# Turning normed rows by plain transpositions of rows that VectorE has scaled, in a two-layer hybrid decoder trunk

## What is computed

```python
def rms_norm(x, gain=None):
    xf = x.astype(jnp.float32)
    y = xf * lax.rsqrt(jnp.mean(xf * xf, axis=-1, keepdims=True) + EPS)
    if gain is not None:
        y = y * gain.astype(jnp.float32)
    return y.astype(x.dtype)

def hybrid_layer(x, ln_mix_pre, w_in, ..., ln_mlp_pre, w_up, w_down, ln_mlp_post):
    h = rms_norm(x, ln_mix_pre)
    ... = split_projection(h @ w_in)
    ...
    x = x + rms_norm(merged @ w_out, ln_mix_post)
    h2 = rms_norm(x, ln_mlp_pre)
    ff = jnp.square(jax.nn.relu(h2 @ w_up)) @ w_down
    return x + rms_norm(ff, ln_mlp_post)
```

## Time and profile before

| | us |
|---|---|
| median of 3 runs | 2002.19 (2001.02 to 2003.47) |
| the profiled execution | 2001.97 |
| its span | 2000.2 |
| TensorE busy | 1928.5 |
| VectorE busy | 1067.6 |
| GpSimd busy | 1024.3 |
| ScalarE busy | 474.2 |

### The profile page before, as it was taken

The page is one execution under the profiler, slowest core; times in us unless marked ns, Lnnn a source line. Parts: engine busy times, 40 slices in busy tenths (PEclk is TensorE's granted clock), DMA queues, the critical chain, the costliest instruction groups (busy, mean ns, idle before and its releaser), DMA issues.

```text
span 2000.2 us, 25269 instructions
## 1 busy us (share of the span) xinstructions
PE 1928.5 (96%) x8926; PEld 1552.1 (78%) x8926; DVE 1067.6 (53%) x1686; ACT 474.2 (24%) x923; POOL 1024.3 (51%) x821
## 2 busy tenths in 40 slices
PE   8999999999999999999999999999999999999998
PEld 7876667788778888888878667677887788888887
DVE  5754798743464550363366547987435646403623
ACT  3153243221323100011222533523113241000111
POOL 5663443335670666666346534342456607666662
PEclk9999999999999999999999999999999999999999
DMA  6332112222520322222222311122125204222321
GB/s 241 133 122 68 56 61 71 80 74 74 200 95 1 138 95 95 95 98 92 84 85 95 127 58 64 63 72 79 64 74 210 84 1 147 94 95 97 102 93 57
DMA packets 72475, 186.77 MB, mean 93 GB/s; under 512 B 18304, under 2 KB 30784, under 8 KB 71488
## 3 DMA queue, kind: packets, MB, share of 16 engines
q1 hardware_dynamic: 41328, 152.10, 22.2%
q10 hardware_dynamic: 31056, 33.38, 5.0%
HBM read 174.40 MB, written 11.06 MB: 93 GB/s over the span
## 4 chain that ended last, share of the span: by engine, by line
PE 77%; DVE 15%; ACT 4%; issue 3%; POOL 1%; DMA 0%; DVEq 0%; SPq 0%; POOLq 0%; ACTq 0%
PE psD L1008 19%; PE psD L1009 19%; PE psD L1010 19%; PE psM L1008 3%; PE psM L1009 3%; PE psM L1010 3%; DVE work L2047 3%; DVE small L2045 3%; PE psM L1067 2%; PE psM L1074 2%; PE psM L1164 1%; PE psM L1172 1%; DVE x L1946 1%; POOL w_lo L982 1%; ACT wide L1508 1%
## 5 line engine op out<-in xcount | busy, mean ns | idle before, releaser
L982 POOL TENSOR_TENSOR w_lo<-raw,w_hi 128x1024 fp32r<-128x1024 f32 x272 | 672.8, 2473 | 22.7
L1008 PE MATMUL psD<-a_hi,w_hi 128*128 128x512 f32 (+2 forms) x1488 | 601.3, 404 | 10.0 <-DVE a_lo L2170 6.6
L1010 PE MATMUL psD<-a_hi,w_lo 128*128 128x512 f32 (+2 forms) x1488 | 578.4, 389 | 0.0
L1009 PE MATMUL psD<-a_lo,w_hi 128*128 128x512 f32 (+2 forms) x1488 | 578.3, 389 | 0.0
L977 POOL TENSOR_TENSOR w_hi<-raw,tabs 128x1 fp32r<-128x1 f32 x272 | 62.7, 230 | 916.9 <-PE psD L1010 806.7
L1008 PEld LDWEIGHTS psD<-a_hi,w_hi 128*128 128x128 f32 (+1 forms) x1488 | 281.9, 189 | 89.8 <-issue 30.2
L1009 PEld LDWEIGHTS psD<-a_lo,w_hi 128*128 128x128 f32 (+1 forms) x1488 | 281.9, 189 | 59.7 <-issue 5.7
L1010 PEld LDWEIGHTS psD<-a_hi,w_lo 128*128 128x128 f32 (+1 forms) x1488 | 281.5, 189 | 58.8 <-issue 0.4
L978 POOL TENSOR_SCALAR w_hi<-raw 128x1023 fp32r<-128x1023 f32 x272 | 297.8, 1095 | 0.0
L2200 DVE TENSOR_TENSOR f_lo<-gt,f_hi 128x512 f32 x64 | 127.4, 1990 | 59.3 <-ACT f_hi L1766 59.3
L1766 ACT CAST f_hi<-gt 128x512 f32 x64 | 39.8, 622 | 479.7 <-DVE gt L2197 479.7
(11 more groups left out here) (268 smaller groups left out, 2720.7 us busy)
## 6 DMA issues: line engine op xcount, KB each, us to landing
raw<-in_ws SPq DMA_DIRECT2D x272, 512.0 KB, 3.2
s_raw<-in_wo ACTq DMA_DIRECT2D x14, 512.0 KB, 11.4
out<-x SPq DMA_DIRECT2D x8, 512.0 KB, 5.5
x<-rows_d ACTq DMA_DIRECT2D x4, 1024.0 KB, 6.8
x<-out ACTq DMA_DIRECT2D x2, 2048.0 KB, 8.2
e_raw<-in_wo ACTq DMA_DIRECT2D x8, 512.0 KB, 6.5
tabs<-in_tab SPq DMA_DIRECT2D x1, 2944.0 KB, 11.4
x<-in_x SPq DMA_DIRECT2D x4, 512.0 KB, 5.3
```

Of the source, the lines that this page charges most:

```text
L982: pool.tensor_tensor(w_lo[:, s, :], raw[:, s, :], w_hi[:, s, :].bitcast(F32), ALU.subtract) \
L1008: pe.matmul(out, lhi, rhi, start=start, stop=False)
L1009: pe.matmul(out, lhi, rlo, start=False, stop=False)
L1010: return pe.matmul(out, llo, rhi, start=False, stop=stop)
```

## The change

`diagonal` becomes `scaled`. VectorE now multiplies the tile of `x` itself by the column of scales, in two halves of 128 by 512, and writes all of `wide[:, t]`; each half raises a semaphore. TensorE turns blocks of `wide` by plain transpositions (a matmul in transpose mode, with the identity as its other operand), and waits for the half that it needs. The order of the halves follows the order in which TensorE turns the blocks: channels 4 to 7 first in front of the projections, save for the last tile, and channels 0 to 3 first everywhere else. In the MLP's turn the wait for the scales moves into the loop over the halves.

```diff
-            def diagonal(norm, t, of=None):
+            def scaled(norm, t, of=None):
 
                 r = rstd(norm, t, 1, of)
-                sig(dve.tensor_scalar(wide[:, t, 0:P], T("ident"), r, None, ALU.mult), "diag_" + norm)
+                for half in (0, 1) if norm == "pre_mlp" or t == ST - 1 else (1, 0):
+                    w = slice(half * S, (half + 1) * S)
+                    sig(dve.tensor_scalar(wide[:, t, w], x[:, t, w], r, None, ALU.mult), "rows_" + norm)
...
         def scaled_T(pe, ps, t, k):
-            return pe.matmul(ps[:, cut(t)], x[:, t, cut(k)], wide[:, t, 0:P], start=True, stop=True)
+            return pe.transpose(ps[:, cut(t)], wide[:, t, cut(k)], T("ident"))
 
         def activation_T(pe):
             for t in range(ST):
-                pe.wait_ge(*on("diag_pre_mix", t + 1))
-                for k in range(KT) if t == ST - 1 else (4, 5, 6, 7, 0, 1, 2, 3):
+                for i, k in enumerate (range(KT) if t == ST - 1 else (4, 5, 6, 7, 0, 1, 2, 3)):
+                    if i % (KT // 2) == 0:
+                        pe.wait_ge(*on("rows_pre_mix", 2 * t + i // (KT // 2) + 1))
...
                     def turn_x1(t):
-                        pe.wait_ge(*on("diag_pre_mlp", t + 1))
                         for i in range(2):
+                            pe.wait_ge(*on("rows_pre_mlp", 2 * t + i + 1))
...
-                                ins = pe.matmul(x1_T(t, k), x[:, t, cut(k)], wide[:, t, 0:P], start=True, stop=True)
+                                ins = pe.transpose(x1_T(t, k), wide[:, t, cut(k)], T("ident"))
```

More of the change, by code:

```diff
@@ L594, in build @@
         per_layer = {"slab_done": NSLAB, "split": NSLAB, "a_hi": (2 + ST) * KT, "a_lo": (2 + ST) * KT,
-                     "h_turned": KT, "r_pre_mix": ST, "diag_pre_mix": ST}
+                     "h_turned": KT, "r_pre_mix": ST, "rows_pre_mix": 2 * ST}
         def sem(name):
@@ L741, in rstd @@
                 return cols[6]
-            def diagonal(norm, t, of=None):
+            def scaled(norm, t, of=None):
                 r = rstd(norm, t, 1, of)
-                sig(dve.tensor_scalar(wide[:, t, 0:P], T("ident"), r, None, ALU.mult), "diag_" + norm)
-            return total, rstd, diagonal
+                for half in (0, 1) if norm == "pre_mlp" or t == ST - 1 else (1, 0):
+                    w = slice(half * S, (half + 1) * S)
+                    sig(dve.tensor_scalar(wide[:, t, w], x[:, t, w], r, None, ALU.mult), "rows_" + norm)
+            return total, rstd, scaled
         def signals(eng, who):
@@ L967, in _ @@
                 seen, sig, own = signals(dve, "dve")
-                total, rstd, diagonal = dve_norm(dve, sig, own)
+                total, rstd, scaled = dve_norm(dve, sig, own)
                 dve.wait_ge(kept["basics_in"], 16)
                 for t in range(ST):
-                    diagonal("pre_mix", t)
+                    scaled("pre_mix", t)
             @block.gpsimd
@@ L2183, in _ @@
                             lo_x1(READY - 1)
-                        diagonal("pre_mlp", t)
+                        scaled("pre_mlp", t)
                         if t == READY - 1:
@@ L2254, in _ @@
                         if t and layer < DEPTH - 1:
-                            diagonal("pre_mix", t - 1, layer + 1)
+                            scaled("pre_mix", t - 1, layer + 1)
                         r = rstd("post_mlp", t, 2)
@@ L2260, in _ @@
                     if layer < DEPTH - 1:
-                        diagonal("pre_mix", ST - 1, layer + 1)
+                        scaled("pre_mix", ST - 1, layer + 1)
                 if layer == DEPTH - 1:
```

## The result

The changed kernel takes 2012.49 us (median of 22 runs) against 2004.3 us for the kernel before (22 runs beside it). The ratio is 1.0036, with a 95% interval of 1.0022 to 1.0049. The forecast was 1998.7 us, 0.17% faster. The profiled execution of the changed kernel took 2016.06 us.

A forecast was written before the change was run, and what follows sets the result against it. TensorE was taken to bound the kernel nearly throughout. MLP 4.4, boundary 1.0, start 0 and clock -2.15 sum to 3.25 us, off the profiled 2001.97: 1998.7 us, range of all cases 1994.8 to 2001.0.

The forecast's parts named there:

- TensorE's turns: Plain transpositions halve each turn's cost: 0.110 us less for each of 128 turns, 14.1 us in all.
- In front of the MLP: Shorter turns of tiles 0, 1 and 3 save 2.2 us a layer, 4.4 for both; bounds 3.2 and 4.4.
- At the boundary: Between the layers, the projection starts some 1.9 us earlier, counted as 1.0 for the half rate; bounds -1.0 and 2.6.
- At the start: Launch start: 0 taken, since later inputs set the projection's start and tile 3's scaling meets GpSimd; bounds -1.0 and 0.8.
- VectorE's scaling: Two 128 by 512 scalings per tile hold VectorE's queue for 0.8 us, each tile 0.6 us longer.
- The clock: Longer gaps cost one more 1.45 us half-rate loss at the MLP and 0.7 us at the start: -2.15 together.
- The half-rate stretches double: Rival, chance 0.05: longer gaps bring longer low-clock stretches at MLPs, start and boundary, losing 8.35 us against 5.4 gained: 2004.9.
- transpositions don't keep the clock up: Rival, chance 0.13: only work after the transpositions raises the clock at boundary and start, leaving 1.7 us gain: 2000.3.
- VectorE and GpSimd meet: Rival, chance 0.07: they delay each other at boundary and start, about 1 us per meeting, leaving 1.25 us gain: 2000.7.
- What would show it: Readings to check: 128 fewer TensorE records, turns 1.75 us, MLP gap about 3.5 us, boundary gap split, half-rate stretches.

The follow-up runs named there:

- e1: The change at pre_mlp (the MLP) alone, diagonal kept at pre_mix, against the kernel before: 2005.47 us, ratio 1.0004.
- f6: The changed kernel plus 24 idle transpositions ahead of tile 3's turn at pre_mix (start and layers' boundary): 2001.1 us, 0.9988 of the kernel before.
- e2: The change at pre_mix (start and layers' boundary) alone, diagonal kept in the MLP, against the kernel before: 2008.17 us, ratio 1.0021.
- e3: The changed kernel, but scaled rows are turned by float32 products with the identity instead of transpositions: 2004.97 us, 1.0009 of the kernel before.
- e4: The changed kernel with each transposition issued twice in a row: 2005.50 us, 1.0008 of the kernel before.
- f7: The changed kernel with 24 idle transpositions in the MLP's wait and 24 ahead of tile 3's turn at pre_mix: 1997.19 us, 0.9966 of the kernel before.
- g8: The kernel before, with the MLP's first two up-projection slabs multiplied for tiles 0 and 1 during the wait, tiles 2 and 3 last: 1987.64 us, ratio 0.9921.

## Why the prediction was wrong, point by point

- **TensorE's turns: right.** 16 turns in 1.66 us (628.45 to 630.11, output tile 3), forecast 1.75; 8798 records.
- **In front of the MLP, 2.2 us a layer: right.** The rows give 1.80 us up to the restart and 0.45 behind tile 3's turn (2.22 against 2.67), and e1 gives 2.6 a layer at an even clock. The gap grew to 3.47 and 3.48 us where 3.5 was put, output tile 3 took 9.65, and VectorE's extra 0.6 us hid, as argued.
- **At the boundary, 1.0: the number is right, half of the working is not.** It was to be a start of the projection some 1.9 us earlier, cut to 1.0 for the half rate. The start came 1.09 us earlier, and the half rate behind it was not in that: it lasted 3.60 us into the projection where it had lasted 1.96. GpSimd was let go earlier, as named, but lost the lead beside x +=, so tile 3's rows came 0.16 us later and not 0.6 earlier; all that was won is the halved turn of tile 3. That the numbers meet is luck.
- **At the start, 0: wrong, about -1.** In f6, where TensorE is at the full rate, the projection starts at 17.64 instead of 16.66. It is the lower bound of the term, reached by the meeting of tile 3's scaling with `w_lo` that was named and left out of the term's middle. Start and boundary together, -1 and 1.09, fit e2's even-clock result, 0 where the sum had 1.0.
- **VectorE's scaling: right.** The pair takes 0.88 us and holds the queue for 0.80 (634.88 to 635.68, where the first `a_lo` begins), forecast 0.8. All of it costs about 1.0 us at the end (e3).
- **The clock, -2.15: the step that failed.** It measured -12.7 (10.8 to 14.7 by the slope). All terms but this one sum to 5.4 in the prediction, and to 4.5 on the chip. The working priced a fall at the 1.45 us of one stretch of 3.41 us that the trace had, and asked only how often it would come. It was the size that changed: 6.83 us in place of 3.41, 10.24 in place of 3.41 or nothing behind the turn of tile 3, where no fall was looked for at all, a whole 6.83 at the start, and 3.41 in each layer behind the wait of 2.12 us that the change did not touch. The reason that was missed: shorter turns and longer waits change the same thing in two ways, TensorE has less to do and more time to stand. The sum credits a saving ahead of a gap with nothing ("it only lengthens the gap"); by e3 and the changed kernel the halved turns as a whole brought 31.4 us more at the half rate, 12.2 us of time for 5.5 saved. Which of the turns brought how much is not shown.
- **The rivals.** The half-rate stretches double had the right mechanism, at 0.05, and 2004.9 for the profiled time; it still left out the 10.24 us behind tile 3's turn. Its argument against itself, that the restarts are dense, fails: the dense stretches are those that pay most for a low clock. That transpositions don't keep the clock up (0.13) is refuted by e3 and e4. That VectorE and GpSimd meet is true at the start, at its price of about 1 us.
- **What would show it** named the right readings; the range, to 2001.0, was too narrow since on the slow side it left the clock's term 2.3 us. The 69 runs of the kernel before alone spread over 32 to 64 us of half-rate time, and from 1998.29 to 2009.57 us.

What stays open: why a single execution falls or not at a given gap. e1 kept the rate behind 3.47 and 3.48 us, and f6 behind one of its two waits of 3.48; the changed kernel lost it for 3.42 us at 602.60, behind a wait of 2.12 us that the kernel before passes at the full rate. That the halved turns cost half-rate time in the mean is shown here, and that filling the waits gives it back; the single stretch isn't explained.

## What to carry to other kernels

Making an engine's work shorter just ahead of its own wait gives nothing, and on TensorE it can cost: here the halved turns brought 31.4 us more at the half rate (the changed kernel against e3). Price the wait that it lengthens, the whole stretch after it, and the dense work in that stretch above all. Read the half-rate time from every run, not from one profile, and compare kernels at an even clock first and by half-rate time second. The remedy is to put work into the wait (other tiles' products that are ready, or, where there are none, transpositions that nobody reads), and with that in place the original saving comes back. The Trainium skill (TensorE: Matmul & The Clock Gate, Part 1, HAM oscillation) advises, for products with few rows whose loop waits on DMA at every tile, to restructure the loop so that TensorE stays at its full clock. g8, a reordering that fills a wait for VectorE, agrees in kind: 0.79% faster for three edited lines, of which 11.2 us less at the half rate are 4.4 us and 11.0 us are the filled wait and the cheaper products.

## What the hardware did that I had not expected

- Work whose result is thrown away made the kernel faster: each transposition issued twice, by 0.28% (e4 against the changed kernel, each by its ratio), and idle transpositions in the gaps by 0.7% (f7).
- The same program differs by 17 us between executions, nearly all by the clock: e1's 12 runs went from 1992.82 us (clock 0.992) to 2009.55 (0.981). Three of them had 32 to 44 us at the half rate, nine 60 to 76, and none lay between.
- The places act on each other over hundreds of microseconds: in f6, filling the waits at pre_mix took 30 us of half-rate time away where e2 had shown only 10 for the change there. That a fall at the start brings falls 600 us later would fit, but it is not shown: the kernel before had its start at the full rate and fell in layer 0's MLP all the same.
- A pair of scalings of 128 by 512 on VectorE took 2.87 us beside GpSimd's `w_lo` (2.34 us), and 0.88 alone.
